# Two layers of a hybrid backbone on one core: the token rows are reloaded between the layers through ScalarE's queue, and the projection weights no longer stand behind them

## What is computed

```python
for i in range(2):
    mod_l = c_act @ mod_w[i] + mod_b[i]              # six vectors a layer, for each stream
    hl = modulate(rms_norm(xl, norm_g[i, 0]), mod_l[:, 0], mod_l[:, 1])
    ...
    xl = xl + mod_l[:, 2] * yl                       # layer 0: conv and pooling; layer 1: attention
    h2l = modulate(rms_norm(xl, norm_g[i, 1]), mod_l[:, 3], mod_l[:, 4])
    ...
    xl = xl + mod_l[:, 5] * moe(h2l, ...)            # 32 experts, top 2 within one of 8 groups
```

## Time and profile before

| | us |
|---|---|
| median of 3 runs | 959.02 |
| lowest and highest run | 958.89, 960.29 |
| the profiled execution | 957.75 |
| its span | 956.0 |
| busy: TensorE matmul, VectorE, GpSimd, ScalarE | 846.6, 323.4, 171.4, 170.0 |
| moved by the DMA engines | 298.00 MB, 312 GB/s on average |

### The profile page before, as it was taken

The page is one execution under the profiler, slowest core; times in us unless marked ns, Lnnn a source line. Parts: engine busy times, 40 slices in busy tenths (PEclk is TensorE's granted clock), DMA queues, the critical chain, the costliest instruction groups (busy, mean ns, idle before and its releaser), DMA issues.

```text
span 956.0 us, 10282 instructions
## 1 busy us (share of the span) xinstructions
PE 846.6 (89%) x3887; PEld 374.0 (39%) x3887; DVE 323.4 (34%) x711; ACT 170.0 (18%) x419; POOL 171.4 (18%) x210
## 2 busy tenths in 40 slices
PE   4899999999999999688759999888899999778785
PEld 2444445447333333222257444354545333222221
DVE  1279997216111211111132431637415111111011
ACT  2301023115000000000032112445414000000000
POOL 2100391221220222220222211300111011011001
PEclk9999999999999999989969999999999999899899
DMA  8999454709999999999898033363657999999993
GB/s 362 409 419 381 164 215 182 304 17 335 340 403 403 371 402 368 422 400 417 355 385 363 0 122 142 154 288 128 282 216 261 395 406 410 415 418 427 410 419 158
DMA packets 33687, 298.00 MB, mean 312 GB/s; under 512 B 6528, under 2 KB 6834, under 8 KB 16220
## 3 DMA queue, kind: packets, MB, share of 16 engines
q1 hardware_dynamic: 26640, 283.26, 73.5%
q0 software_dynamic: 6912, 13.92, 4.1%
q10 hardware_dynamic: 76, 0.02, 0.0%
HBM read 293.66 MB, written 12.58 MB: 320 GB/s over the span
## 4 chain that ended last, share of the span: by engine, by line
PE 45%; DMA 22%; DVE 15%; issue 6%; SPq 5%; ACT 4%; PEld 2%; POOL 1%; another core or an unknown queue 0%; PEldq 0%; POOLq 0%; DVEq 0%; ACTq 0%
PE bank L1250 12%; DMA ring<-in_gu_pack 11%; DVE WORK L2149 9%; PE bank L473 9%; PE bank L1273 5%; PE bank L1398 5%; SPq L965 3%; DMA ring<-in_win_pack 3%; DMA ring<-in_down_pack 3%; PE bank L1128 3%; PE bank L1345 2%; DMA WORK<-x_old,smalli 1%; DVE small L1784 1%; PE bank L1024 1%; DMA h_rows<-B 1%
## 5 line engine op out<-in xcount | busy, mean ns | idle before, releaser
L1250 PE MATMUL bank<-ring,hT 128*64 128x512 f32 x688 | 208.2, 633 | 27.5 <-DMA ring<-in_gu_pack 20.2
L2063 DVE SCALAR_TENSOR_TENSOR hT<-hT,WORK,bank 128x256 f32<-128x256 f32 x34 | 16.3, 480 | 327.5 <-ACT hT L1549 327.5
L1250 PEld LDWEIGHTS bank<-ring,hT 128*64 128x64 f32 x688 | 61.8, 145 | 123.5 <-issue 123.3
L2149 DVE SCALAR_TENSOR_TENSOR WORK<-WORK,par 128x512 f32<-128x512 f32 x116 | 90.7, 862 | 0.0
L473 PE MATMUL bank<-ring,hT 128*128 128x512 f32 (+2 forms) x256 | 88.0, 499 | 0.7 <-ACT hT L1512 0.7
L1273 PE MATMUL bank<-ring,WORK 128*64 128x512 f32 x368 | 83.5, 596 | 3.6 <-DMA ring<-in_down_pack 3.2
L1554 ACT ACTIVATE WORK<-bank 128x256 f32<-128x256 f32 x34 | 13.1, 384 | 282.3 <-PE bank L1259 282.3
L1250 PE MATMUL bank<-WORK,hT 128*64 128x512 f32 x128 | 58.2, 596 | 4.6 <-issue 3.0
L473 PEld LDWEIGHTS bank<-ring,hT 128*128 128x128 f32 x256 | 46.0, 190 | 35.8 <-issue 34.0
L1345 PE MATMUL bank<-hT,ring 128*128 128x512 f32 x128 | 57.7, 610 | 2.0 <-DMA ring<-in_win_pack 2.0
L1250 PE MATMUL bank<-X,hT 128*64 128x512 f32 x112 | 53.7, 627 | 6.0 <-DMA B<-in_gu_pack 4.5
(11 more groups left out here) (297 smaller groups left out, 1035.0 us busy)
## 6 DMA issues: line engine op xcount, KB each, us to landing
ring<-in_gu_pack SPq DMA_DIRECT2D x38, 2048.0 KB, 22.4
ring<-in_mod_pack SPq DMA_DIRECT2D x24, 2048.0 KB, 13.2
ring<-in_down_pack SPq DMA_DIRECT2D x22, 2048.0 KB, 27.8
WORK<-in_gu_pack SPq DMA_DIRECT2D x6, 2048.0 KB, 31.4
ring<-in_wout_pack SPq DMA_DIRECT2D x4, 2048.0 KB, 16.3
ring<-in_gu_pack SPq DMA_DIRECT2D x8, 1024.0 KB, 27.9
ring<-in_win_pack SPq DMA_DIRECT2D x3, 2048.0 KB, 37.0
X<-in_gu_pack SPq DMA_DIRECT2D x3, 2048.0 KB, 30.1
```

The source lines that it names most:

```text
L1250: mm = pe.matmul(dst[ST * x:ST * x + ST, :], HG[L][s][:, k, :], columns(units[x], 512 * k, 512), start=k == 0, stop=k == KC - 1)
L2063: dve.scalar_tensor_tensor(out=T1[L][s], in0=SG[L][s], scalar=cwt[:, at:at + 1], in1=src[:, 0:DE], op0=ALU.mult, op1=ALU.mult).then_inc(se ...
L2149: ins = dve.scalar_tensor_tensor(out=acc, in0=src, scalar=w, in1=acc, op0=ALU.mult, op1=ALU.add)
```

## The change

SP no longer waits for `moe_done` and no longer reloads X. ScalarE does both, after its part of layer 0's experts and before the first squares of layer 1. The four transfers, their order and their semaphores are the same. The projection units, which came behind the reload in SP's queue, are now held only by their places in the ring.

```diff
@@ -979,11 +979,6 @@
                     for i in range(NT):
                         tokens = a[("ctx", "x")[i // 2]][0].rearrange("(i p) d -> i p d", p=P)
                         sp.dma_start(X[:, i, :], tokens[i % 2]).then_inc(sem("x_in"), 16)
-                if u == ('oin', 'ckv'):
-
-                    sp.wait_ge(sem("moe_done"), 1)
-                    for t in range(NT):
-                        sp.dma_start(X[:, t, :], xb[t * P:(t + 1) * P, :]).then_inc(sem(f"x_back_{t // 2}"), 16)
                 load(n, load_sources(u) if u[0] not in ("gu", "down") else expert_sources(u[1], u[2], n, u[0]))
 
             sp.wait_ge(sem("x_saved"), 96)
@@ -1657,6 +1652,9 @@
             raw_cols(0, 1, 0)
             square_rows("m0", (3,))
             moe_scalar(act, 0, moe_gate_rows, hcols, experts)
+            act.wait_ge(sem("moe_done"), 1)
+            for t in range(NT):
+                act.dma_start(X[:, t, :], xb[t * P:(t + 1) * P, :]).then_inc(sem(f"x_back_{t // 2}"), 16)
             square_rows("a1", (0, 1))
             mod_copy(7)
             square_rows("a1", (2, 3))
```

## The result

| | before | after |
|---|---|---|
| median of 4 runs, us | 958.95 | 982.81 |
| lowest and highest | 957.77, 960.29 | 978.33, 986.10 |
| profiled execution, us | 957.75 | 981.78 |
| its span, us | 956.0 | 980.0 |

What follows compares the result with a forecast made beforehand. The seam between the layers was taken as a latency chain through the token rows, not weight loads. X's second half 21.7 us later plus 0.5 for the clock gave 980.0 profiled, 981 as median with 1.3 added; range 966 to 987.

Steps and rivals of the forecast that it cites:

- The weights run ahead: SP's queue before layer 1: ckv issued near 441, all five projection units by 469, lora and a modulation half at 479.
- They are worth nothing on the path: Projection weights issued early gain none, because no row has TensorE waiting for them.
- The last scatters: End of layer 0: they meet a full DMA queue, the last takes 8.5 us, `moe_done` comes 5.2 us later; bounds 0 and +7.5.
- The reload: X on ScalarE's queue alternates packet by packet with SP's weights; last tile lands at 508.5, 21.7 us later than before.
- the second rival: Reload of X is not interleaved but served behind all that SP issued before it: 982 to 986 us; chance 10%.
- From X to the projections: Squares, norm steps and transposes between X's last landing and L473: their 10.1 us stay.
- 0.5 for the clock: TensorE's low clock after standing still may reach into the first projections: 0 to 3 us, taken as 0.5.
- The shift passes to the end one for one: A later start of TensorE's projections at L473 delays the kernel's end by the same amount, through layer 1.
- even sharing: The two hardware queues share bytes evenly during X's reload, or X suffers less than GpSimd's queue: +7.4, 966.4 us; chance 12%.
- That the weights would not run ahead: SP held at a slot wait past `moe_done`, X lands as today: 959 us, no change; 5%, including small packets spared, 956.

Runs made afterwards that it cites:

- act_alone: Changed kernel, but SP waits until all four tiles of X have landed before issuing the first projection unit; 959.04 us, ratio 0.9991 to the kernel before.
- two_ahead: Kernel before, but only ckv and ql go ahead of SP's wait on `moe_done` and the reload; 961.45 us, ratio 1.0030.
- small_packets: Changed kernel, same bytes and order, but projection units, lora and a modulation half loaded in rows of 2.5 to 4 KB; 969.14 us.
- same_time: Changed kernel, but SP also waits for `moe_done` before the first projection unit, so both queues start together; 972.18 us, ratio 1.0142 to the kernel before.
- split: Kernel before, but the reload is issued from two queues, X tiles 0 and 1 by ScalarE, 2 and 3 by SP; 962.94 us, ratio 1.0026.
- split_even: Kernel before, but the reload is issued from two queues, X tiles 0 and 2 by SP, 1 and 3 by ScalarE; 958.94 us, ratio 0.9980.
- split_tiles: Kernel before, with X tiles 0 and 2 from SP, 1 and 3 from ScalarE, a wait per tile, `mod_copy(7)` ahead of the squares; 959.94 us, ratio 0.9994.

## Why the prediction was right

The forecast was 981, in 966 to 987; the median is 982.81. The profiled execution came out at 981.78 where the sum, 980.0, was made for it. Point by point:

- **The weights run ahead.** Right: ckv at 441.25, all five units issued by 469.6, lora at 479.80, where 441, 469 and 479 were forecast.
- **They are worth nothing on the path.** Right. In act_alone the five units are issued 18 to 43 us later than in the changed kernel and the time is that of the kernel before; in two_ahead they fill the hole and it costs 0.3%.
- **The last scatters: +5.2, with +7.5 as the upper bound.** Measured 6.28 (9.56 for 3.28; X is first issued 6.65 us later, since the scatter also went out 0.36 us later). The mechanism was right, the size a little small: I had gone to the short end because ckv's and ql's rows are small, and for the data of the scatters that held. What I had left out stands in the DMA view of 480 to 484 of the changed kernel: GpSimd's queue has 60 packets with next to no bytes, beside 115 of SP's that average 14.8 KB, kd's rows:

```profile
q1 hardware_dynamic: 115, 1.70, 100.6%
q0 software_dynamic: 60, 0.00, 1.1%
```

The scatter ends with many tiny packets, and if each of them waits for a turn too, it pays for the size of the packets beside it. In small_packets, whose turns are short, the same scatter took 6.0 us, which fits; the tiny packets were not tried by themselves.
- **The reload: from its first issue, near 483.1, to the last landing at 508.5, 25.4 instead of 8.9 us.** Measured 25.25 (484.58 to 509.83), +16.4. That the total is so near is partly luck. The forecast had data 0.9 us after the issue and then 24.5 us; measured are 3.4 us to the first packet and 21.8 from there. The turns are right, and the views of the changed kernel and of same_time show them, 178 to 176 and 503 to 499; that a part of SP's loads goes ahead of the first packet, as in the second rival, the forecast had left to that rival alone. Nor was every packet of X paired: from 505 to 507 there are 72 of X's queue and 33 of SP's. The counts of the earlier trace rows were of GpSimd's queue; that ScalarE's is served alike was an assumption in the forecast and is now measured. The Trainium skill (DMA: Bandwidth & Descriptors, Queues, rings and completion order) has the turns by packet; the counts agree. The preferred packet of at most 4096 B stands on the same page of the Trainium skill (SWDGE vs HWDGE vs iDMA) in its table on the descriptors that GpSimd builds, and the prediction stretched it when it tried it on SP's weight rows. small_packets, where these rows really are so small, is the kernel in which the queues share evenly.
- **From X to the projections: 10.1 us stay, and 0.5 for the clock.** 10.25 us were measured. The clock cost the projections nothing: the first 48 matmuls of L473 take 8.04 us in both kernels.
- **The shift passes to the end one for one.** Right: 23.15 us at L473, 24.0 in the span. The rest, some 0.85 us, arises in layer 1's experts, with a lower granted clock in one stretch. Before and after, the same work, 23.15 us apart (the columns as in the earlier trace rows):

```profile
715.00:760.00 45.00, 42.72 (x276) 21.78 (x276) 17.34 (x75) 12.53 (x28) 5.01 (x7) 1.00 0.86 308
```

```profile
738.15:783.15 45.00, 43.23 (x274) 23.35 (x274) 16.92 (x74) 12.63 (x28) 5.00 (x7) 0.96 0.83 301
```

Of the rivals, even sharing (966) is refuted for these row sizes by same_time and the counts. The queue served in order of issue would have given nearly the same time for the changed kernel, as was said, so the 982.81 us alone doesn't tell the two apart; what refutes it, but for the 3.4 us ahead of the first packet, is small_packets and the interleaved packets themselves. That the weights would not run ahead is refuted by SyncE's timeline.

What stays open is what delays the first packet of X by 3.4 us. The spread of the times says nothing: the four runs of the changed kernel lie within 7.8 us and those of the kernel before within 2.5, but over 29 runs on another chip the kernel before spreads over 7.8 us too (955.20 to 962.97).

## What to carry to other kernels

A hole in the DMA engines' time is not a loss while a small transfer on the critical path lies next to it: what fills the hole competes with that transfer. Before giving loads a free run, look whether any engine ever waits for them, and ask which latency chain crosses the stretch that they will fill. A second queue doesn't shelter a transfer: here the queues took turns by packet, and the one with 4 KB rows beside one with rows of up to 16 KB got 22% of the bytes; hold the large loads behind the small transfer, put them in narrower rows, or issue the parts so that what is needed first stands at the head of every queue. Of these only the first gave the old time back here (act_alone, 959.04 us); narrower rows left 969.14.

## What the runs showed that I had not expected

- **The clock at the end of the seam doesn't follow the length of the idle time.** In the traces of two_ahead, split, split_even and split_tiles the granted clock is still 0.50 (1.2 GHz) when the projections begin, and their first 48 matmuls take 9.83, 9.90, 9.95 and 9.95 us, against 8.04 or 8.05 in the other seven kernels, the changed one among them, whose idle time was the longest of all. It is a cost of 1.8 to 1.9 us, as large as the gains that the last four kernels were after; a seam of 18.3 us has it in split_even and one of 18.4 us has it not in act_alone. What decides it was not tried, and with one trace for each kernel it can't be said whether it belongs to the kernel or to the single execution.
- **One queue of 4 KB rows doesn't fill the engines.** X alone in ScalarE's queue moves at 314 GB/s (act_alone, 477.5 to 484), in two queues at 410 GB/s (split, 482 to 487, 1.02 MB from one and 1.03 from the other). It fits that the last tile lands 7.8 us after the first issue in split_even and 8.9 us in the kernel before; that this made the 0.2% was not shown.
